# Two small mixers in a diffusion block: when the convolution's chunks are rounded, which query panels come first, and which engine evicts values

## What is computed

```python
def token_mixer(hl, hc, w_in, q_norm_w, kv_norm_w, w_uq, w_ukv, conv_w, w_out, tabs, ctx_out):
    cq_l, ckv_l, kpe_l, gb_l, gc_l, xv_l = jnp.split(hl @ w_in, IN_SPLITS, axis=-1)
    ...
    k_c, v_c = mla_keys_values(ckv_c, kpe_c, kv_norm_w, w_ukv, None)
    k_l, v_l = mla_keys_values(ckv_l, kpe_l, kv_norm_w, w_ukv, tabs)
    q_l = mla_queries(cq_l, q_norm_w, w_uq, tabs)
    k_all = jnp.concatenate([k_c, k_l], axis=1)
    v_all = jnp.concatenate([v_c, v_l], axis=1)
    att_l = blocked_attend(q_l, k_all, v_all).reshape(b, l, MLA_OUT)
    conv_l = gb_l * short_conv(gc_l * xv_l, conv_w)
    out_l = jnp.concatenate([att_l, conv_l], axis=-1) @ w_out
    if not ctx_out:
        return out_l, None
    q_c = mla_queries(cq_c, q_norm_w, w_uq, None)
    att_c = attend(q_c, k_c, v_c).reshape(...)
    conv_c = gb_c * short_conv(gc_c * xv_c, conv_w)
```

## Time and profile before

| | us |
|---|---|
| time, median of 3 runs | 4516.12 (4515.93 to 4524.71) |
| time of the profiled execution | 4522.2 |
| span of the profiled execution | 4520.4 |
| PE busy | 4294.9 (95%) |
| DVE busy | 3221.8 (71%) |
| ACT busy | 1825.0 (40%) |
| POOL busy | 1423.2 (31%) |
| mean granted PE clock | 0.973 of full |

### The profile page before, as it was taken

One profiled execution on the slowest core, in us unless ns is written; L12 is line 12 of the kernel. 1 busy time (PEld: TensorE's weight loads), 2 busy tenths in 40 slices (PEclk: granted clock), 3 DMA queues, 4 the chain that ended last, 5 costly groups with the idle time before them and its releaser, 6 DMA issues.

```text
span 4520.4 us, 62059 instructions
## 1 busy us (share of the span) xinstructions
PE 4294.9 (95%) x24455; PEld 3842.2 (85%) x24455; DVE 3221.8 (71%) x5137; ACT 1825.0 (40%) x2986; POOL 1423.2 (31%) x701
## 2 busy tenths in 40 slices
PE   7999899999999998999999899799999999999999
PEld 5887678887888798767899899799998799999887
DVE  5764547876887575464589899498886757785776
ACT  3233242233233434254233577233334544444444
POOL 0000300000000100000277688667772028665443
PEclk9999999999999998998999999899999999999999
DMA  6543214544544264201467799899995146678884
GB/s 269 221 158 124 75 38 177 223 177 184 226 184 183 93 246 169 79 34 47 133 218 236 244 331 330 289 373 351 359 352 181 39 166 220 211 243 275 288 288 163
DMA packets 286689, 926.50 MB, mean 205 GB/s; under 512 B 19136, under 2 KB 170816, under 8 KB 212288
## 3 DMA queue, kind: packets, MB, share of 16 engines
q1 hardware_dynamic: 249536, 788.30, 49.1%
q0 software_dynamic: 36864, 134.23, 8.4%
HBM read 837.52 MB, written 84.93 MB: 204 GB/s over the span
## 4 chain that ended last, share of the span: by engine, by line
PE 77%; DVE 12%; DMA 5%; ACT 3%; POOL 2%; issue 1%; SPq 0%; DVEq 0%; ACTq 0%; POOLq 0%
PE bank L1032 22%; PE bank L1034 21%; PE bank L1033 21%; DVE work L2356 3%; PE bank L1203 2%; PE bank L1397 2%; DMA gates<-work 2%; PE bank L1018 2%; PE bank L1187 2%; PE bank L1022 1%; PE bank L1094 1%; DMA work<-in_up_rows,work 1%; DVE work L2463 1%; POOL weight_ring_low L2611 1%; PE bank L1194 1%
## 5 line engine op out<-in xcount | busy, mean ns | idle before, releaser
L2611 POOL TENSOR_TENSOR weight_ring_low<-weight_ring,up_high 128x1024 fp32r<-128x1024 f32 x240 | 650.2, 2719 | 1138.4 <-ACT up_high L1761 1136.4
L1034 PE MATMUL bank<-peer_h_high,weight_ring_low 128*128 128x256 f32 (+2 forms) x2240 | 702.7, 314 | 0.0
L1032 PE MATMUL bank<-peer_h_high,up_high 128*128 128x384 f32 (+1 forms) x2048 | 648.5, 317 | 35.6 <-POOL weight_ring_low L2611 33.7
L1033 PE MATMUL bank<-h_low,up_high 128*128 128x384 f32 (+1 forms) x2048 | 638.2, 312 | 0.0
L1032 PE MATMUL bank<-h_high,in_high 128*128 128x512 f32 (+1 forms) x1280 | 465.3, 364 | 5.6 <-DVE weight_ring_low L2002 5.2
L1848 ACT ACTIVATE down_high<-weight_ring 128x1024 fp32r<-128x1024 f32 x256 | 257.4, 1054 | 517.0 <-PE bank L1034 511.5
L1034 PE MATMUL bank<-h_high,weight_ring_low 128*128 128x512 f32 (+1 forms) x1280 | 464.7, 363 | 0.0
L1033 PE MATMUL bank<-h_low,in_high 128*128 128x512 f32 (+1 forms) x1280 | 464.6, 363 | 0.0
L2578 POOL TENSOR_SCALAR h<-work,params 128x256 f32<-128x256 f32 x12 | 10.9, 921 | 1439.8 <-DVE work L2266 1439.8
L1034 PEld LDWEIGHTS bank<-peer_h_high,weight_ring_low 128*128 128x128 f32 x2240 | 429.8, 192 | 3.8
L1032 PEld LDWEIGHTS bank<-peer_h_high,up_high 128*128 128x128 f32 x2048 | 394.3, 193 | 40.6 <-POOL weight_ring_low L2611 38.3
(11 more groups left out here) (364 smaller groups left out, 10527.3 us busy)
## 6 DMA issues: line engine op xcount, KB each, us to landing
weight_ring<-in_up SPq DMA_DIRECT2D x128, 1024.0 KB, 5.6
weight_ring<-in_down SPq DMA_DIRECT2D x128, 1024.0 KB, 6.6
weight_ring<-in_mod_w SPq DMA_DIRECT2D x112, 1024.0 KB, 5.4
weight_ring<-in_ffn_in SPq DMA_DIRECT2D x88, 1024.0 KB, 6.8
weight_ring<-in_ffn_out SPq DMA_DIRECT2D x64, 704.0 KB, 4.4
gates<-work SPq DMA_DIRECT2D x40, 1024.0 KB
gelu<-work SPq DMA_DIRECT2D x64, 384.0 KB
work<-gates SPq DMA_DIRECT2D x16, 1536.0 KB
```

Of the source, the lines that this page charges most:

```text
L1032: mm(dst, w_high, a_high, start=first, stop=False)
L1033: mm(dst, w_high, a_low, start=False, stop=False)
L1034: return mm(dst, w_low, a_high, start=False, stop=last)
L2611: G.tensor_tensor(ring_low[:, slot, w], ring[:, slot, w], up_high[:, n % 3, :].bitcast(F32), ALU.subtract)\
```

## The change

Five edits, all in the two mixers of the first block.

1. The rotary query panels come first: panels 18 and 19 are now the rotary rows, 20 to 23 the plain rows, on PE and on DVE. POOL's start condition is as it was written, so that it now waits until DVE has emptied the first rotary panel.
2. The margin in `projections` goes: the PE waits only until the bank that it needs is empty.
3. ACT copies the unrotated context rows of the rotary query panels (in `mix_0` alone), under a new semaphore `context_copied`, and DVE waits for it before it rotates that panel.
4. ACT copies the four value panels, after the keys, under a new semaphore `values_copied`. The PE waits for it between the first four score tiles and the first transpose, not before the scores. DVE goes from the plain query rows straight to the first maximum.
5. The convolution's four chunks are rounded one a step: on ACT in steps 19 to 22 of `mix_0` and 3 to 6 of `mix_1`, each at the end of the step, the first behind the wait for `conv_ready`; and split two steps later on DVE. The order in which chunks enter the output projection is the same.

```diff
@@ peer, counts @@
-                counts["free"] += 28
+                counts["free"] += 24
                 counts["keys"] += 4
+                counts["context"] += 2 * (s["t"] == T)
@@ PE, projections @@
-                    pe.wait_ge(bank_free, f0 + p - 3)
+                    pe.wait_ge(bank_free, f0 + p - BANKS + 1)
@@ PE, mix_stage @@
-                p = projections(name, plan.unit0[f"uq_{l}"], [(0, 2 * c, 2, mla_cq, t) for c in range(6)], f0, p)
+                p = projections(name, plan.unit0[f"uq_{l}"], [(0, 2 * c, 2, mla_cq, t) for c in (4, 5, 0, 1, 2, 3)], f0, p)
...
-                pe.wait_ge(bank_free, f0 + p - HEADS // 2)
-                attention(name)
+                pe.wait_ge(bank_free, f0 + p - HEADS)
+                attention(name, lambda: pe.wait_ge(values_copied, at[name]["keys"] + 4))
@@ ACT, attention @@
+                first = 4 * min(pairs) + 3
...
-                    if i == 4 and before:
+                    if before and first <= i < first + len(before):
                         act.wait_ge(conv_ready, at[name]["conv"] + 1)
-                        for kc in before:
-                            round_part(name, kc)
+                        round_part(name, before[i - first])
@@ ACT, mix_stage @@
+                if t == T:
+                    for c in range(2):
+                        act.wait_ge(panel_done, plan.panel0[name] + 18 + c + 1)
+                        for j in range(4):
+                            i = A(mla_q[NOPE:QK, 4 * c + j, CTX], ps[(18 + c) % BANKS][ROPE * j:ROPE * j + ROPE, CTX], ACT.Copy)
+                        i.then_inc(context_copied, 1)
                 for hd in range(HEADS):
...
+                for tt in range(4):
+                    act.wait_ge(panel_done, plan.panel0[name] + 28 + tt + 1)
+                    A(mla_v[:, tt, :], ps[(28 + tt) % BANKS][:, :], ACT.Copy).then_inc(values_copied, 1)
@@ DVE, attention @@
+                first = 4 * min(pairs) + 3
...
-                    if i == 6:
-                        for kc in before:
-                            split_part(name, kc)
+                    if before and first + 2 <= i < first + 2 + len(before):
+                        split_part(name, before[i - first - 2])
@@ DVE, mix_stage @@
+                for c in range(2):
+                    p = 18 + c
+                    arrived(name, p)
+                    if t == T:
+                        dve.wait_ge(context_copied, at[name]["context"] + c + 1)
+                    a, b = rope(name, p, slice(0, P), ROPE // 4, cos, sin)
+                    for j in range(4):
+                        rows = slice(ROPE * j, ROPE * j + ROPE)
+                        i = V.tensor_tensor(mla_q[pe_rows, 4 * c + j, LAT], a[rows], b[rows], ALU.add)
+                    i.then_inc(bank_free, 1)
                 for hd in range(HEADS):
-                    p, half = 18 + hd // 2, slice(hd % 2 * NOPE, hd % 2 * NOPE + NOPE)
+                    p, half = 20 + hd // 2, slice(hd % 2 * NOPE, hd % 2 * NOPE + NOPE)
...
-                for tt in range(4):
-                    arrived(name, 28 + tt)
-                    V.tensor_copy(mla_v[:, tt, :], ps[(28 + tt) % BANKS][:, :]).then_inc(bank_free, 1)
```

More of the change, by code:

```diff
@@ L455, in build @@
         bank_free, keys_copied = sem("bank_free"), sem("keys_copied")
+        context_copied, values_copied = sem("context_copied"), sem("values_copied")
         lora_ready, conv_input, conv_ready = sem("lora_ready"), sem("conv_input"), sem("conv_ready")
@@ L507, in build @@
         counts = dict(norm=0, added=0, ffn=0, free=4, square=0, root=0, lora=0, conv=0, tile=0, out=0, mod=0,
-                      peer=0, ptile=0, rtile=0, parts=0, scaled=0, normed=0, rounds=0, keys=0)
+                      peer=0, ptile=0, rtile=0, parts=0, scaled=0, normed=0, rounds=0, keys=0, context=0)
         take = scratch()
@@ L2268, in mix_stage @@
                         i.then_inc(bank_free, 1)
-                for c in range(2):
-                    p = 22 + c
-                    arrived(name, p)
-                    four = [(4 * c + j, slice(ROPE * j, ROPE * j + ROPE)) for j in range(4)]
-                    for hd, rows in four:
-                        if t == T:
-                            steps.count(V.tensor_copy(mla_q[pe_rows, hd, CTX], ps[p % BANKS][rows, CTX]))
-                    a, b = rope(name, p, slice(0, P), ROPE // 4, cos, sin)
-                    for hd, rows in four:
-                        i = V.tensor_tensor(mla_q[pe_rows, hd, LAT], a[rows], b[rows], ALU.add)
-                    i.then_inc(bank_free, 1)
-                for tt in range(4):
-                    arrived(name, 28 + tt)
-                    V.tensor_copy(mla_v[:, tt, :], ps[(28 + tt) % BANKS][:, :]).then_inc(bank_free, 1)
                 steps.wait()
```

## The result

The changed kernel takes 4495.04 us, the median of 5 runs (4489.84 to 4498.18); the kernel before, on the same chip, 4517.45 (5 runs, 4515.93 to 4524.71). The ratio is 0.9949, 95% interval 0.9937 to 0.9960: 22 us faster (18 to 28), with 4491.5 predicted. The profiled execution spans 4493.2 us, against 4520.4.

A forecast was written before the change was run, and what follows sets the result against it. PE was busy 95% of the span, so only its stalls and low-clock stretches in the two mixers counted; -14.8 + 1.3 - 7.6 - 3.5 = -24.6 us from the 4516.12 median gave 4491.5 us, range 4484 to 4503.

The forecast's parts named there:

- The wait for the convolution: mix_0 attention: late rounding removes ScalarE's 10.2 us wait for GpSimd and the half clock after it, -14.8 us.
- The roundings and splits among the tiles of 256 keys: mix_0: four roundings and splits moved among the tiles with 256 keys cost +1.3 us (0.5 to 5.0).
- the row I priced them by: mix_0, earlier trace: next group after 2.73 us behind one rounding and split, against 2.48 without; 0.25 us each.
- mix_0's front: Edits 1 to 4 in mix_0: no PE stalls, first scores at full clock, second group near 530.8 instead of 538.41, -7.6 us.
- mix_1: Edits 1, 2, 4 and 5 there: earlier scores, full clock, partly lost to a convolution wait; -3.5 us (-2.4 to -5.0, or 0).
- The sum: Whole kernel: -14.8 + 1.3 - 7.6 - 3.5 = -24.6 us, giving 4491.5 us; nothing moves outside the two mixers.
- The clock did not fall between 526 and 565: Sign in mix_0's attention: the prediction is wrong if the clock is 0.5 anywhere between 526 and 565.
- the rival: Clock falls elsewhere: up to 3.7 us more in mix_0, 1 to 3.5 less gain in mix_1; sum -17 to -20; chance 0.25.
- a sign that I had named for being wrong: mix_0, behind step 19: the prediction is wrong if groups with 256 keys go to 3 us and more.
- The convolution stays the late one: mix_0: convolution ends after 565, only if VectorE's work slows GpSimd; at 5 us late, sum -15, 4501 us; chance 0.05.

The follow-up runs named there:

- late rounding alone: Kernel before with only the convolution's roundings and splits moved late, one a step; old panel order and eviction engines; ratio 0.9975 to before.
- experiments 10 and 11: Unmodified repeats for second profiles: the changed kernel (ratio 0.9952 to before), then the kernel before (mix_0 88.61 us, mix_1 55.03 us to the last turning back).
- experiment 9: Changed kernel with the first rounding at step 14 in mix_0 and step 5 in mix_1, GpSimd's start untouched; median 4493.12 us, ratio 0.9945 to before.
- experiment 7: Kernel before with late rounding, GpSimd's convolution held until both rotary panels are freed; one run, to last turning back 73.16 us in mix_0, 59.98 in mix_1.
- experiment 6: Changed kernel with GpSimd's convolution allowed to start one freed bank earlier; one run, to last turning back 67.42 us in mix_0, 54.54 in mix_1.
- experiment 2: Changed kernel with the four roundings back in one block in step 4 and splits in step 6; ratio 0.9993 to before.
- experiment 4: Changed kernel with VectorE copying the context rows of the rotary panels again; one run, mix_0 first scores at 9.71 us against 6.86.

## Why the prediction was right

**The wait for the convolution**, -14.8 us predicted. From the second group of scores to the group at 569.66 in the earlier trace rows it is 31.25 us, now 547.42 - 530.89 = 16.53: -14.7. The late rounding alone shows the same 16.54. The convolution ends at 553.41 + 5.52 = 558.93, near the 558.3 worked out, and the first rounding is at 566.51: 7.6 us of margin for the 7 predicted.

**The roundings and splits among the tiles of 256 keys**, +1.3 predicted. The group at 577.03 has lost 1.25 us. But the row I priced them by, 0.25 us for each rounding, does not describe what happened: nothing is lost up to 570.38, then 0.55 and 1.15 in two steps, the larger where two splits of VectorE meet (before, this part had a loss of its own, the 2.73 in the earlier trace rows, so the net is less). In the late rounding alone all of it is still there at the last turning back, 9.81 us after that group (9.82 before). In the changed kernel it is 9.28 us, so 0.5 is regained; but that is the low clock coming later, for the turning back at 583.27 took 0.39 us and its like before, at 604.31, took 0.64, and it is paid behind the last one (experiments 10 and 11). The size was right partly by luck.

**mix_0's front**, -7.6 predicted. The second group of scores is 8.0 us earlier against the first key panel. First scores at 526.43 (526 predicted), table load at 527.60 (527.5). The load takes 1.28 us, as in the earlier trace rows, and ends where the first exponential begins, 528.89. The Trainium skill (ScalarE: Activation LUTs, What ACT_TABLE_LOAD costs) splits its 2.7 us into a load of about 1.28 and a drain of about 1.38: the trace agrees with the first and shows nothing of the second, since 1.3 us pass from the last value copy's end to the exponential. The 0.4 us missed are the value copies, 2.06 us for four and not 4 x 0.61: back to back they follow each other every half microsecond.

**mix_1**, -3.5 predicted. Measured -4.3 against the first profile of the kernel before and -3.4 against the second; the 0.9 between them is how long the clock stayed low. The end of the convolution was right: 28.06 us after the first query panel, which is 1507.8 in the profile before (1507.7 predicted). Three other steps were off. The idle time lies before the last key panel, not the first value panel: that key panel's bank is the second rotary panel's, which I had counted as one panel later. ScalarE's wait was 4.6 us, not 2.7: it asks at 1488.23 - 4.57 = 1483.66, which is 1503.2 in the profile before; I had put 1505.4, read off from a copy of step 4, while the first rounding is due in step 3. Of the wait 1.1 us reached TensorE (experiment 9 takes it away), where I let 1.35 through, so this miss cost nothing. And the cause was incomplete: I priced the first rotation's additions without GpSimd beside them, but did not see how much its start decides. Started later in the old order, it gives 3.3 of the 4.5 us at the second group (experiment 7); started earlier in the new one, it takes 4.0 of them back (experiment 6).

**The sum**: mix_0 -22.0 (-21.1 predicted), mix_1 -3.4 to -4.3 (-3.5), together -25 to -26 with -24.6 predicted. The prediction took everything outside the two mixers as unmoved. It is not: with the code between them, from mix_0's first key panel to mix_1's last turning back, the gain is 24.3 us by the first profiles and 24.9 by the second ones. The first profiles differ by 27.2 and the medians by 22.4. The code behind mix_1 takes 2972.6 to 2987.1 us over the thirteen profiles and 3.3 less in the changed kernel's first profile than in that of the kernel before, with no order by kernel, so that the 3.5 us between 4491.5 and 4495.04 say nothing for or against a term.

**The rivals.** The clock did not fall between 526 and 565 (1.00), and in mix_1 not behind the 1.81 us of idle time. It did fall elsewhere in a small way: behind mix_0's last turning back it was low for longer, at 1.1 us by the first wait, where the rival had up to 3.7. The Trainium skill (TensorE: Matmul & The Clock Gate, Why this matters for your kernels) warns of idle gaps between bursts of matmuls only from a length on that the gaps here hardly reach; the clock fell behind 2.92 us in experiment 6 and also behind 2.48 in the kernel before. The groups of 256 keys did reach 3.0 and 3.6 us, a sign that I had named for being wrong; it was two groups, not the whole stretch. "The convolution stays the late one" is what the front alone does (experiment 2), where the rounding stands in step 4; it needed no slower GpSimd.

## What to carry to other kernels

Before you price an edit that makes work arrive earlier, find the next gate on the path and ask who opens it: two halves of an edit were worth 11 and 3 us apart and 22 us together. Moving a wait behind work that doesn't need its data gave the same, whichever engine evicted the data. Measure past the end of the stretch that you changed: half a microsecond of mix_0's gain was only a low clock that came later. And when a reordering delays a neighbour engine's start, test that delay by itself, since it may be the larger part of the gain, and then check who waits for the neighbour at its end.

## What the chip showed that I had not expected

- VectorE's additions of two operands in SBUF, 32x256, take 1.71 us for four with GpSimd idle, 2.06 to 2.15 beside GpSimd's first pass (scalar multiplications), and 2.26 to 2.76 beside its later ones (multiplications and additions in turn). The first pass takes 3.64 us (four rows) beside VectorE's copies out of PSUM, 4.12 beside the second rotation, and 5.63 beside the 32x4096 copy within SBUF and the first rotation (GpSimd early). The copies were not slowed: 3.52 us for eight of 64x256 with GpSimd beside them or not.
- In mix_1 TensorE was idle for 1.81 us and then ran at a granted clock of 1.00; after 2.92 us at the same place it was 0.59 over the next 7.4 us. With idle times of 0.92 and 1.44 us (experiment 7) the first scores ran at full speed; with 2.49 and 1.44, in the late rounding alone, the clock over them was 0.75. Five idle times of 0.3 us between pairs of matmuls (experiment 4) cost some 0.57 us each and left the clock at 1.00; the 0.57 is the idle time and the 0.26 by which a pair of 1.12 us outlasts the 0.86 at which pairs follow each other without a wait.
- The low clock did not last equally long behind the same idle times: mix_1's first four tiles took 6.27 us in one profile of the kernel before and 5.37 in the other, mix_0's 5.55 and 7.10.
